# Scan of a state-space block: the gated norm's reciprocal and scaling spread over three later steps, and the state products issued ahead of those with mT

## The reference

```
for each group g:
    for each chunk c:
        mT[h]   = scores(c, c)^T * decay(h)                 # 128x128 per head
        y_diag  = mT[h] @ xdt[h]                            # xdt = x * dt
        y_off   = C(c) @ state * exp(a_cs)                  # not for c = 0
        state   = state * chunk_decay + B(c)^T @ xdec       # xdec = x * decay to the chunk's end
        y       = y_diag + y_off + d_skip * x
    y = y * silu(z)
    y = y / sqrt(mean over the group's 512 channels of y^2 + eps) * ssd_norm_w     # gated norm
y_ssd = y @ w_branch_ssd
```

## Time and profile before

| | |
|---|---|
| median of 3 runs | 2546.71 us (2544.07 to 2549.95) |
| the profiled execution | 2534.87 us; span 2533.0 us, mean granted TensorE clock 0.974 |
| PE busy | 2392.3 us, 94% of the span |
| DVE busy | 1386.4 us, 55% |
| ACT busy | 1062.3 us, 42% |
| POOL busy | 394.1 us, 16% |
| chain that ended last | PE 81%, DVE 7%, ACT 4%, DMA 3%, issue 3% |

### The profile page before, as it was taken

How to read it: one execution, slowest core, us unless ns; L and a number is a source line. 1 busy time by engine, 2 the same in 40 slices (tenths; PEclk the granted TensorE clock), 3 DMA queues, 4 the chain that set the end, 5 groups by cost and what they waited for, 6 DMA issues and landing times.

```text
span 2533.0 us, 41300 instructions
## 1 busy us (share of the span) xinstructions
PE 2392.3 (94%) x15423; PEld 2136.3 (84%) x15423; DVE 1386.4 (55%) x2101; ACT 1062.3 (42%) x1908; POOL 394.1 (16%) x350
## 2 busy tenths in 40 slices
PE   5899988999899999998989999999999989999998
PEld 4678867887689889886868999999878779999987
DVE  5886675423455335457854666643343445766621
ACT  5545863433544234323544433322455545333322
POOL 0000433711320010000121211100100001211100
PEclk8898998999999999999999999999999989999999
DMA  8464332332333353342201323333422112323332
GB/s 279 137 213 116 101 83 59 91 100 75 100 93 91 97 130 98 92 119 52 64 21 48 99 85 89 91 89 89 125 60 62 50 47 80 87 87 91 89 93 92
DMA packets 409384, 238.35 MB, mean 94 GB/s; under 512 B 11338, under 2 KB 400301, under 8 KB 409285
## 3 DMA queue, kind: packets, MB, share of 16 engines
q1 hardware_dynamic: 400453, 202.24, 28.7%
q0 software_dynamic: 8224, 32.61, 3.8%
q10 hardware_dynamic: 608, 2.16, 0.2%
HBM read 234.53 MB, written 5.00 MB: 95 GB/s over the span
## 4 chain that ended last, share of the span: by engine, by line
PE 81%; DVE 7%; ACT 4%; DMA 3%; issue 3%; POOL 0%; SPq 0%; DVEq 0%; POOLq 0%; ACTq 0%
PE PS L507 60%; PE PS L2033 5%; PE PS L1820 3%; DMA w_raw<-in_w_in_dram 1%; DVE ada_acc L617 1%; PE PS L1775 1%; PE PS L2164 1%; PE PS L2069 1%; PE PS L1835 1%; PE PS L2111 1%; ACT w_hi L428 1%; PE PS L1899 1%; DVE w_lo L434 1%; DVE conv_acc L2275 1%; DMA w_ada<-in_w_ada_dram 1%
## 5 line engine op out<-in xcount | busy, mean ns | idle before, releaser
L434 DVE TENSOR_TENSOR w_lo<-w_raw,w_hi 128x1024 fp32r<-128x1024 f32 (+1 forms) x376 | 474.4, 1262 | 637.7 <-ACT w_hi L428 636.5
L507 PE MATMUL PS<-op_hi,w_hi 128*128 128x264 f32 (+4 forms) x2456 | 608.2, 311 | 22.4 <-DVE w_lo L434 11.4
L507 PE MATMUL PS<-op_lo,w_hi 128*128 128x264 f32 (+4 forms) x2456 | 605.3, 310 | 0.0
L507 PE MATMUL PS<-op_hi,w_lo 128*128 128x264 f32 (+4 forms) x2456 | 603.0, 309 | 0.0
L428 ACT ACTIVATE w_hi<-w_raw 128x1024 fp32r<-128x1024 f32 (+1 forms) x376 | 382.8, 1018 | 313.5 <-PE PS L507 261.4
L507 PEld LDWEIGHTS PS<-op_hi,w_hi 128*128 128x128 f32 (+1 forms) x2456 | 399.6, 189 | 56.2 <-DVE w_lo L434 11.3
L507 PEld LDWEIGHTS PS<-op_hi,w_lo 128*128 128x128 f32 (+1 forms) x2456 | 398.9, 189 | 24.6 <-issue 0.8
L507 PEld LDWEIGHTS PS<-op_lo,w_hi 128*128 128x128 f32 (+1 forms) x2456 | 398.7, 189 | 23.4 <-issue 1.4
L507 PE MATMUL PS<-ff_hi,w_lo 128*128 128x512 f32 (+1 forms) x784 | 240.3, 343 | 0.0
L507 PE MATMUL PS<-ff_hi,w_hi 128*128 128x512 f32 (+1 forms) x784 | 239.9, 342 | 0.0
L507 PE MATMUL PS<-ff_lo,w_hi 128*128 128x512 f32 (+1 forms) x784 | 239.9, 342 | 0.0
(11 more groups left out here) (486 smaller groups left out, 3828.6 us busy)
## 6 DMA issues: line engine op xcount, KB each, us to landing
w_raw<-in_w_up_dram SPq DMA_DIRECT2D x120, 512.0 KB, 3.9
w_raw<-in_w_in_dram SPq DMA_DIRECT2D x64, 512.0 KB, 4.1
w_raw<-in_w_down_dram SPq DMA_DIRECT2D x64, 512.0 KB, 4.0
w_ada<-in_w_ada_dram POOLq DMA_DIRECT2D x12, 2048.0 KB, 10.3
decay<-sums_scratch SPq DMA_DIRECT2D x16, 512.0 KB, 5.1
w_raw<-in_w_branch_ssd_dram SPq DMA_DIRECT2D x16, 512.0 KB, 4.0
w_raw<-in_w_in_a_dram SPq DMA_DIRECT2D x16, 512.0 KB, 3.8
w_raw<-in_w_kv_b_dram SPq DMA_DIRECT2D x16, 512.0 KB, 3.9
```

The lines of the kernel that those rows point to most:

```text
L434: dve.tensor_tensor(wlo[slot][:, 0:ks, :], wraw[slot][:, 0:ks, :], whi[slot][:, 0:ks, :].bitcast(F32), ALU.subtract).then_inc(sem("w_split ...
L507: last = pe.matmul(a[0:l.cols, h, 0:cn], w[slot][:, k, 0:l.cols], x[:, kk, c0:c0 + cn], start=(j == 0 and k == 0 and w is whi and x is l.h ...
```

## The change

DVE: the reciprocal of group gg moves from the end of step 9 + 4 gg into step 10 + 4 gg, behind mT and w_lo and in front of the wait for `ssd_bd`. The scaling of its four tiles moves to the same place in the next two steps, two tiles in each; for the last group, the first two tiles follow the reciprocal at step 22 and the other two are at step 23. PE: `C @ state` and `B^T @ xdec` are issued before the mT products; they wait for `ssd_b` and for xdec (`ssd_xd`) instead of mT, and `ssd_bd` is given by the last mT product. The instructions are the same in number and size.

```diff
                 if i < 16:
+                    pe.wait_ge(sem("ssd_b"), i + 1)
+                    pe.wait_ge(sem("ssd_xd"), 2 * i + 2)
+                    if c > 0:
+                        pe.matmul(bank(5), cT[:, g, cs], stt_[:], start=True, stop=True)
+                    if c < 3:
+                        pe.matmul(bank(4), btok[:], xdec[:], start=True, stop=True)
                     pe.wait_ge(sem("ssd_m"), i + 1)
-                    pe.wait_ge(sem("ssd_b"), i + 1)
                     for h in range(HPG):
                         last = pe.matmul(bank(1)[:, h * HDIM:(h + 1) * HDIM], mT[:, h, :],
                                          xdt[:, h * HDIM:(h + 1) * HDIM], start=True, stop=True)
-                    if c > 0:
-                        last = pe.matmul(bank(5), cT[:, g, cs], stt_[:], start=True, stop=True)
-                    if c < 3:
-                        last = pe.matmul(bank(4), btok[:], xdec[:], start=True, stop=True)
                     last.then_inc(sem("ssd_bd"), 1)
...
                 split_lo(dve, l_, g_ // 2, g_ % 2, 0)
+                if i >= 10:
+                    gg, part = (i - 10) // 4, (i - 10) % 4
+                    rg = (rs if gg % 2 == 0 else vt[1])[:, 0:S]
+                    if part == 0:
+                        dve.wait_ge(sem("gn_std"), gg + 1)
+                        link(dve.reciprocal(rg, rg))
+                    tiles = ((), (0, 1), (2, 3), ())[part] if gg < 3 else ((0, 1), (2, 3))[part]
+                    for j in tiles:
+                        j = 4 * gg + j
+                        dve.scalar_tensor_tensor(zT[:, j, :], zT[:, j, :], pcol("ssd_norm_w", j), rg, ALU.mult,
+                                                 ALU.mult).then_inc(sem("y_v"), 1)
                 if i < 16:
                     dve.wait_ge(sem("ssd_bd"), i + 1)
...
-                if i >= 9 and (i - 9) % 4 == 0:
-                    gg = (i - 9) // 4
-                    rg = (rs if gg % 2 == 0 else vt[1])[:, 0:S]
-                    dve.wait_ge(sem("gn_std"), gg + 1)
-                    link(dve.reciprocal(rg, rg))
-                    for j in range(4 * gg, 4 * gg + 4):
-                        dve.scalar_tensor_tensor(zT[:, j, :], zT[:, j, :], pcol("ssd_norm_w", j), rg, ALU.mult,
-                                                 ALU.mult).then_inc(sem("y_v"), 1)
```

## The result

The changed kernel takes 2520.58 us (median of 5 runs, 2517.06 to 2527.07), the kernel before beside it 2544.07 us (5 runs, the three shown above among them; 2536.98 to 2549.95). The ratio is 0.9914, with a 95% interval of 0.9887 to 0.9941: 22 us faster, give or take 7. A second series on another occasion gave 0.9935 (0.9921 to 0.9950), 16.5 us. The forecast was 2530 us, in a range of 2521 to 2541; the saving was put at 16 us.

The account below looks back on a forecast made before the run. PE's work plus its waits was taken to bound the kernel. A ceiling of 22.4 us less 5.0 in the scan and 1.2 at the end gave 16.2 us, off 2546.7: forecast 2530 us, range 2521 to 2541.

Parts of the forecast that it names:

- The ceiling: Scan and u units: PE's waits for mT and w_lo, 13.2 us, plus slow-clock loss, 9.2 us; 22.4 us in all.
- Part 3: State products first on PE: fill 0.9 to 1.8 us of waits for mT, already in the sums; elsewhere nothing.
- Part 1: Steps 10 and 14: without norm work before mT, PE's wait and slow stretch go; step 10's last product ends at 331.6.
- Part 2: Steps 10 to 15: norm work in the ACT and DVE loop delays mT, costing 5.0 us, bounds 0 to about 9.
- step 14's wait for the root: Step 14: ACT's late table load and root hold PE about 1.6 us instead of 0.87, costing 0.7 us.
- The rival that built on it: DVE and POOL exclude each other at each tile pair, steps 11 and 12: saving 9.2 us, 2537.5; chance 0.15.
- Part 4: Queues passed: SP's decay load for step 13 lands at 345.3, ACT wants it at 347.7; cost 0, 2 us cover.
- Part 5: u units: the 3.8 us w_lo wait goes; late last tiles make PE wait 1.2 us before the third gate unit.
- X: The end of u unit 7; the last y_lo was forecast to end 8.3 us after it, before 5.2.
- The rival of the falling clock: Clock falls at six new short waits, 3.4 to 4.1 us each; with all six 6.3 us slower, 2553; chance 0.03.
- The level: Saving taken off the runs' median, 2546.7 us, which lay 11.8 us above the profiled execution; gives 2530.5, forecast 2530.

Follow-up runs that it names:

- experiment 3: Changed kernel without the norm's reciprocal and 16 scalings on DVE: ratio 0.9914 to the kernel before, 23.7 us saved up to the gate units.
- experiment 4: Changed kernel with reciprocal and tile pairs in front of w_lo, last group at the end of step 21: ratios 0.9911 and 0.9917, 24.0 and 24.1 us saved.
- experiment 9: Changed kernel with only the reciprocals of steps 10, 14, 18 before w_lo, last group at the end of step 21: 23.1 us saved, one execution.
- experiment 8: Changed kernel without POOL's squares and running sums for three of each group's four tiles: 19.1 us saved up to the gate units, one execution.
- experiment 2: Changed kernel with PE's old order, mT products before state products: ratio 0.9949 to the kernel before, 11.0 us saved up to the gate units.
- experiment 5: Changed kernel once more, no edit: ratio 0.9935 to the kernel before, 18.4 us saved up to the gate units.
- experiment 6: Changed kernel with only the last group's reciprocal and scalings back at the end of step 21: ratio 0.9921 to the kernel before, 20.0 us saved.
- experiment 1: Kernel before with only PE's new order, state products before mT products: ratio 0.9975, 10.3 us saved up to the gate units.

## Why the prediction was right, and where it was off

**The ceiling** (22.4 us): right. With no norm work 23.7 us are saved; of the 1.3 us above the ceiling 0.6 lie in step 0 and 0.2 each in steps 8 and 12, where state products first help (Part 3).

**Part 1** (the norm away from mT): right. Step 10 takes 12.26 us, the sum had 331.6 - 319.4 = 12.2; the slow stretches are gone.

**Part 2** (the loop of ACT and DVE): the mechanism is shown by experiments 3, 4 and 9, and the terms were near. x_tok of step 10 is 2.2 us behind PE (2.3 forecast). The excess of the steps 11, 12, 13, 14 and 15 is 1.2, 1.4, 0.1, 0.1 and 1.7 us in the first profile (1.2 in the second), 4.5 in all, against 1.1, 1.8, 0.3, 0.7 and 1.1, 5.0 in all. The term that was most mis-sized is step 14's wait for the root, 1.0 us instead of 1.6. I had let ACT be as late as DVE in step 13; but ACT's part from x_tok to the end of w_hi takes 5.4 us in the changed kernel, not the 5.7 of the earlier trace rows, where it also waited a little for PE's unit.

**The rule of exclusion.** The Trainium skill, "SBUF — State Buffer", section "Who interferes with whom", says that a VectorE instruction with two SBUF inputs and a GpSimd instruction that reads SBUF shut each other out, the later one waiting for the whole of the other. The trace agrees: w_lo of step 11 takes 1.96 us with POOL's running sum beside it and 1.23 without (experiment 8). It struck w_lo of steps 11 and 15, mT of steps 12 to 14 and the tile pair of step 15 (2.47 us for two, by the rows of the result), not the pairs of steps 11 and 12 (1.4). The measured price is 0.7 us in step 12 by experiment 8. The rival that built on it, with every pair struck, did not come about.

**Part 3** (state products first): here two sentences were wrong. "Their new conditions, b_tok and xdec, are there before" doesn't hold for xdec in steps 11 and 15, where PE waits 0.36 and 0.83 us for it and then 0.3 us each for mT; so of a wait for mT there only a part is filled. And "Where PE doesn't wait it gives nothing" overlooked that mT is just late in step 0 and in step 8. There the state product now fills the wait: 0.9 us and 0.2 us, the largest part of the 1.8 us by which the saving of 18.0 exceeds my 16.2. And the worth of this half was underrated where PE does wait: I gave it 0.9 us for each of three steps; experiment 2 shows 7.0 us, some 5.1 of them by the clock (half of the slow stretches, an estimate).

**Part 4** (queues): here "0, with 2 us of cover" was wrong by a little. The lateness of mT in step 13 delays the issue of the next decay rows, and in the first profile ACT waited 0.6 us for them in step 14. This was not hidden: it is the 0.5 us by which step 15 is longer there than in the second (experiment 5).

**Part 5** (the tail): right. The last y_lo ends at X + 8.0 (X + 8.3 forecast), PE waits 1.4 us (1.2 forecast), and experiment 6 gives back 1.6. (The last u unit was evacuated at 432.5 us, where the forecast had about 435; this is the larger saving in the scan.)

**The rival of the falling clock** did not come about in the changed kernel (1.00 from 230 to 432 us). But my evidence against it was weaker than I took it to be. The same eight-unit stage of the earlier trace rows, which had the full clock before, has 0.84 in the changed kernel's profile:

```profile
611.00:633.00 22.00, 14.65 (x45) 9.51 (x43) 14.28 (x15) 16.76 (x23) 1.27 (x1) 0.84 0.20 57
```

and in experiment 2 the clock fell behind waits no longer than 1.8 us. With the state products first the waits for mT are at most 1.0 us and the clock stays up, and I hadn't counted that. That it is the length of the waits that decides is not shown: the wait of 1.36 us before gate unit 2 of the changed kernel left the clock at 1.00, one of 1.16 us in experiment 2 did not.

**The level.** I took the saving off 2546.7 us, the median of three runs; five runs have 2544.1, and the longer series 2540.1 and 2541.2. Of the 9.4 us between 2530 and 2520.6, 2.6 are this, 1.8 the larger saving in the trace, and the other 5 are within the interval of the ratio (7 us either way). I had no reason for them and the second series doesn't show them: 2526.7 against 2541.2 us.

## What to carry to other kernels

When work is moved off a critical wait, look where its engine is idle and for what. Here VectorE was idle just in front of w_lo, waiting for ScalarE, and not behind it; directly in front of w_lo the same work cost nothing. In the place chosen it cost 5.7 us: 3.1 for the reciprocal and 1.0 for the tile pairs, by a loop through a buffer that ScalarE reuses, and 1.6 at the end, where the last group's scaling delays the first gate unit's evacuation (experiments 9, 4 and 6). And a half of a change that only fills waits can be worth more than its duration: 7.0 us here, most of them, by the estimate of experiment 2, from slow stretches that don't come.

## What I had not expected of the hardware

The clock does not follow the length of the last wait alone. Two waits of 3.3 us in steps 10 and 14 of experiment 1 left it at 1.00, and so did a wait of 1.75 us in step 11 of experiment 2; waits of 1.16 and 1.75 us in steps 12 and 15 of the same kernel were followed by 3.4 and 6.8 us at 0.50. The 3.8 us wait before u unit 4 had a slow stretch in both kernels that have it, the kernel before and experiment 1; in the latter it began inside the wait. What else PE had done just before differs between these places; the runs don't separate it. The stretch from 1100 to 1300 us, untouched by the change, had a mean clock of 0.95, 0.87 and 0.93 in three profiled executions, and the part behind the gate units took 1992 to 2008 us in the profiled executions of all kernels. That is nearly as much as the whole change is worth, and it hides the change when single executions are compared.
